# Split fp32r products for q, k, v, gate values and u in a decoder step, with the split input kept in scratch

## The reference

```
h = x * (1.0 + sc1) + sh1
z = h @ w_in
q, k, v, f, u, gv, ga, gg = split(z)         # 512, 512, 512, 8, 512, 512, 1024, 1024 columns
logf = log_sigmoid(f + b_f)
u = gelu(u);  gv = layernorm(gelu(gv))
a = fox(q, k, v, logf)                       # attention with forget gates, paged cache for the samples
gm = u * (ws @ gv + b_s)                     # spatial gate in chunks of 128 tokens
m = (sigmoid(ga) * (a @ w_ao) + sigmoid(gg) * (gm @ w_go)) @ w_o
x = layernorm(ALPHA * x + (1.0 + g1) * m)
out = layernorm(ALPHA * x + (1.0 + g2) * moe(x * (1.0 + sc2) + sh2))
```

## Time and profile before

| | |
|---|---|
| median of three runs | 1812.11 us (1808.1 to 1812.4) |
| the profiled execution, its own time | 1809.96 us |
| its span in the profile | 1807.8 us |
| mean granted TensorE clock | 0.944 |
| PE busy, DVE busy, ACT busy, POOL busy | 87%, 48%, 31%, 14% |
| modulate | 0 to 46 us |
| project_in | 46 to 300 us |
| gmlp | 304 to 385 us |
| attend | 389 to 880 us |
| mix | 882 to 1188 us |
| mixer_out, route, experts, combine | 1188 to 1808 us |

### The profile page before, as it was taken

The page is one execution under the profiler, slowest core; times in us unless marked ns, Lnnn a source line. Parts: engine busy times, 40 slices in busy tenths (PEclk is TensorE's granted clock), DMA queues, the critical chain, the costliest instruction groups (busy, mean ns, idle before and its releaser), DMA issues. The chain is left out here.

```text
span 1807.8 us, 32157 instructions
## 1 busy us (share of the span) xinstructions
PE 1580.4 (87%) x11702; PEld 1101.8 (61%) x11702; DVE 870.4 (48%) x1311; ACT 566.9 (31%) x965; POOL 244.2 (14%) x230
## 2 busy tenths in 40 slices
PE   5999998958999999998599998979952899999965
PEld 3444444647776767765399998944431567676731
DVE  2011111924565555555354645434344666766638
ACT  1000002102444444444234334300010556665622
POOL 0001010031001010000121313103231111111021
PEclk9999999978999999999699999989985999999987
DMA  8634443046999989996356464552113899999954
GB/s 331 236 119 166 156 154 94 18 160 229 362 326 322 335 296 334 310 306 208 102 134 186 124 183 124 139 199 70 47 50 143 316 378 419 419 418 418 404 186 183
DMA packets 226254, 411.60 MB, mean 228 GB/s; under 512 B 18844, under 2 KB 112221, under 8 KB 217942
## 3 DMA queue, kind: packets, MB, share of 16 engines
q1 hardware_dynamic: 208392, 345.44, 55.0%
q0 software_dynamic: 13152, 47.95, 7.4%
q10 hardware_dynamic: 4608, 16.78, 2.3%
HBM read 367.26 MB, written 42.85 MB: 227 GB/s over the span
## 5 line engine op out<-in xcount | busy, mean ns | idle before, releaser
L326 PE MATMUL ps<-w_w,h_hT 128*128 128x512 f32 x512 | 227.4, 603 | 7.5 <-issue 4.0
L1527 PE MATMUL ps<-mix_x_hi,mix_w_hi 128*128 128x352 f32 x576 | 188.5, 327 | 25.3 <-DVE mix_x_lo L1479 21.8
L2209 DVE TENSOR_TENSOR ex_w_lo<-we_w_gu,ex_w_hi 128x1024 fp32r<-128x1024 f32 x128 | 150.8, 1220 | 103.1 <-ACT ex_w_hi L2254 102.5
L1527 PE MATMUL ps<-mix_x_hi,mix_w_lo 128*128 128x352 f32 x576 | 187.2, 325 | 0.0
L1527 PE MATMUL ps<-mix_x_lo,mix_w_hi 128*128 128x352 f32 x576 | 186.5, 324 | 0.0
L326 PEld LDWEIGHTS ps<-w_w,h_hT 128*128 128x128 f32 x512 | 97.1, 192 | 126.7 <-issue 125.3
L2254 ACT CAST ex_w_hi<-we_w_gu 128x1024 fp32r<-128x1024 f32 x128 | 128.5, 1061 | 94.8 <-DMA we_w_gu<-w_exp_up 87.0
L976 PE MATMUL ps<-g_ident,at_k_pg 128*128 128x128 f32 x1024 | 140.8, 281 | 15.9 <-DVE at_kT L1163 15.8
L976 PEld LDWEIGHTS ps<-g_ident,at_k_pg 128*128 128x128 f32 x1024 | 115.5, 143 | 63.2 <-issue 38.6
L1569 DVE TENSOR_TENSOR mix_w_lo<-g_arena,mix_w_hi 128x1024 fp32r<-128x1024 f32 x73 | 125.7, 1753 | 41.0 <-ACT mix_w_hi L1554 28.1
L1163 ACT COPY at_kT<-ps 128x512 f32<-128x512 f32 x128 | 74.9, 585 | 179.1 <-PE ps L976 179.1
(11 more groups left out here) (386 smaller groups left out, 2337.0 us busy)
## 6 DMA issues: line engine op xcount, KB each, us to landing
at_k_pg<-cache_k SPq DMA_DIRECT2D x256, 256.0 KB, 4.1
at_v_pg<-cache_v SPq DMA_DIRECT2D x256, 256.0 KB, 4.2
we_w_gu<-w_exp_gate SPq DMA_DIRECT2D x32, 1024.0 KB, 8.9
we_w_gu<-w_exp_up SPq DMA_DIRECT2D x32, 1024.0 KB, 11.2
we_w_dn<-w_exp_down SPq DMA_DIRECT2D x32, 1024.0 KB, 8.1
g_arena<-w_in SPq DMA_DIRECT2D x49, 512.0 KB
h_extra<-w_ada SPq DMA_DIRECT2D x16, 1024.0 KB
y_rows<-ex_y ACTq DMA_DIRECT2D x32, 512.0 KB, 7.5
```

Of the source, the lines that this page charges most:

```text
L326: last = nc.tensor.matmul(ps[:, b, :], g.hT[:, k, t * P:(t + 1) * P], w[s][:, k, :], start=(k == 0), stop=(k == KD - 1))
L1527: last = nc.tensor.matmul(out, w[p][:, at], v[:, x, :], start=(i == 0 and k == 0), stop=(i == len(w_chunks) - 1 and k == 2))
L2209: nc.vector.tensor_tensor(w_lo[half][:, i], w_gu[s][:, i, half * KH:(half + 1) * KH, :], w_hi[half][:, i].bitcast(F32), ALU.subtract).then ...
```

## The change

**Operands.** An operand of a product is split on chip into `hi`, its value rounded to fp32r, and `lo`, the fp32 difference, itself rounded. An fp32 matmul `h @ w` becomes three fp32r matmuls: h_hi x w_hi, h_hi x w_lo and h_lo x w_hi. This is done for the prompt tiles of q, k, v and gv and for all of u. The sample tiles of the four groups stay one fp32 product of the raw operands. The forget logits stay fp32 and are computed as h_hi @ w_f + h_lo @ w_f, sixteen rounds of matmuls in place of eight.

**project_in.** `g.hT` becomes `g.h` with both parts; the lo part is written over the raw values (`twin` makes the same bytes visible in both types). ACT rounds h a tile at a time and the weights in four pieces of two chunks, DVE subtracts. The weights of the next group are split during the last four tiles of a group. The two weight buffers hold hi and lo, and u's weights are a fifth group that goes through them. `g.z` has two slots in place of four, so v waits for q's stores and gv for k's. The `Fori` loop is gone. The sample tile of a group is computed in the middle of the group before it, ahead of the split (that of q at the very start). SP issues the weights of group g+1 when the last tile of group g-1 is done. The ada rows are stored a piece at a time.

The core of the diff (renamings and moved buffers left out):

```diff
 # project_in, SP
-for it in range(2):
-    for s, (at, by) in enumerate(((COL_Q, COL_V - COL_Q), (COL_K, COL_GV - COL_K))):
-        if it or s:
-            sp.wait_ge(w_used[s], START + it)
-            sp.dma_start(w[s][:], w_v[:, :, it * by + at:it * by + at + 512]).then_inc(w_in[s], 16)
-        for a in range(A):
-            x, use, column = piece(it, s, a)
-            sp.wait_ge(ada_added[x], START + use)
-            sp.dma_start(ada_w[x][:, :, :], ada_v[:, :, bass.ds(2 * D + column, PIECE)]).then_inc(ada_in[x], 16)
...
+for gi in range(GROUPS):
+    s = (gi + 1) % 2
+    if gi:
+        sp.wait_ge(w_used[s], (gi + 1) // 2)
+    sp.dma_start(g.w_raw[s][:, 1], w_v[:, :, GROUP_COLS[gi + 1]:GROUP_COLS[gi + 1] + 512])\
+        .then_inc(w_in[s], 16)
+    for n in range(A * gi, A * gi + A):
+        x = n % 2
+        if n >= 2:
+            store_ada(n - 2)
+        sp.dma_start(ada_w[x], ada_v[:, :, 2 * D + n * PIECE:2 * D + (n + 1) * PIECE]).then_inc(ada_in[x], 16)
...
 # project_in, PE, a prompt tile
-for k in range(KD):
-    last = nc.tensor.matmul(ps[:, b, :], g.hT[:, k, t * P:(t + 1) * P], w[s][:, k, :],
-                            start=(k == 0), stop=(k == KD - 1))
+if gi == 0:
+    pe.wait_ge(h_lo_done, t + 1)
+for k in range(KD):
+    if t == 0 and k % 2 == 0:
+        pe.wait_ge(w_lo_done, CH * gi + k // 2 + 1)
+    for i, (h, w) in enumerate(((h_hi, w_hi), (h_hi, w_lo), (h_lo, w_hi))):
+        last = nc.tensor.matmul(ps[:, b, :], h[:, k, tokens(t)], w[:, k, :], start=(k == 0 and i == 0),
+                                stop=(k == KD - 1 and i == 2))
...
+if t % 2:
+    a = A * gi + t // 2
+    x = a % 2
+    pe.wait_ge(ada_in[x], 32 * (a // 2) + 32)
...
 # project_in, POOL
-for j in range(3):
-    pool.dma_start(g.hT_rows[:, j], g.hT[:, :, j * BLK:(j + 1) * BLK]).then_inc(out, 16)
+pool.wait_ge(h_lo_done, NT)
+for part, src in enumerate((h_hi, h_lo)):
+    for j in range(3):
+        pool.dma_start(g.hT_rows[part, :, j], src[:, :, j * BLK:(j + 1) * BLK]).then_inc(h_out, 16)
...
 # gmlp, PE, forget logits
-for j in range(3):
-    last = nc.tensor.matmul(ps[32 * j:32 * j + H, 6, 0:BLK], w_f[:, k, :],
-                            g.hT[:, k, j * BLK:(j + 1) * BLK], start=(k == 0), stop=(k == KD - 1))
+for part in range(2):
+    for j in range(3):
+        last = nc.tensor.matmul(ps[32 * j:32 * j + H, 6, 0:BLK], w_f[:, k, :],
+                                g.h[:, part, k, j * BLK:(j + 1) * BLK].bitcast(F32), start=(k == 0 and part == 0),
+                                stop=(k == KD - 1 and part == 1))
...
 # mix, POOL
+def load_h(j):
+    if j >= 2:
+        pool.wait_ge(w_used[1], START + KD * (j - 1))
+    for part in range(2):
+        pool.dma_start(h_x[j % 2][:, part], g.hT_rows[part, :, j]).then_inc(h_in[j % 2], 16)
 def block_start(j):
-    for q in (1, 2, 3):
-        split_lo(pool, nc.gpsimd.tensor_tensor, q, j)
+    split_lo(pool, nc.gpsimd.tensor_tensor, 1, j)
+    if j < 2:
+        load_h(j + 1)
```

More of the change, by code:

```diff
@@ L1 @@
+import math
 from contextlib import ExitStack
@@ L8 @@
 F32 = mybir.dt.float32
+F32R = mybir.dt.float32r
 I32 = mybir.dt.int32
@@ new lines, in evacuate @@
+            def evacuate(eng, copy, n):
+                gi, t = GROUP_TILES[n]
+                b, slot = n % 6, gi % 2
+                if gi == 2 and t in (0, 1, PT):
+                    eng.wait_ge(q_out, 16 * (1 + H // 2))
+                if gi == 3 and t in (0, 1, PT):
+                    eng.wait_ge(k_out, 16 * (2 + H // 2))
+                eng.wait_ge(full[b], n // 6 + 1)
+                if t == PT - 1:
+                    eng.sem_inc(w_used[gi % 2], 1)
+                if t < PT:
+                    last = copy(g.z[:, slot, t, :], ps[:, b, :])
+                else:
+                    for j in range(4):
+                        last = copy(g.z[0:NS, slot, t, j * P:(j + 1) * P], ps[NS * j:NS * j + NS, b, 0:P])
+                last.then_inc(free[b], 1)
@@ L375, in add_bias, with h_rest, w_rest @@
                     last.then_inc(ada_added[x], 1)
-                evacuate(dve, nc.vector.tensor_copy, 0, add_bias)
+                def h_rest(t):
+                    dve.wait_ge(h_hi_done, t + 1)
+                    nc.vector.tensor_tensor(h_lo[:, :, tokens(t)], raw(t),
+                                            h_hi[:, :, tokens(t)].bitcast(F32), ALU.subtract).then_inc(h_lo_done, 1)
+                def w_rest(gi, c):
+                    at = slice(2 * c, 2 * c + 2)
+                    if gi < GROUPS and c == 0:
+                        n = GROUP_TILES.index((gi, PT))
+                        dve.wait_ge(full[n % 6], n // 6 + 1)
+                    dve.wait_ge(w_hi_done, CH * gi + c + 1)
+                    nc.vector.tensor_tensor(g.w[gi % 2][:, 1, at], g.w_raw[gi % 2][:, 1, at],
+                                            g.w[gi % 2][:, 0, at].bitcast(F32), ALU.subtract).then_inc(w_lo_done, 1)
@@ new lines, in _ @@
+                w_rest(0, 0)
+                h_rest(0)
+                for c in range(1, CH):
+                    w_rest(0, c)
+                for t in range(1, 4):
+                    h_rest(t)
+                for n, (gi, t) in enumerate(GROUP_TILES):
+                    if n % 2 == 0:
+                        evacuate(dve, nc.vector.tensor_copy, n)
+                    if t == PT:
+                        continue
+                    if t % 2:
+                        add_bias(A * gi + t // 2)
+                    if gi == 0 and t + 4 < NT:
+                        h_rest(t + 4)
+                    if t >= PT - CH:
+                        w_rest(gi + 1, t - PT + CH)
@@ new lines, in _ @@
+                h_round(0)
+                for c in range(1, CH):
+                    w_round(0, c)
+                for t in range(1, 4):
+                    h_round(t)
+                for n, (gi, t) in enumerate(GROUP_TILES):
+                    if n % 2:
+                        evacuate(act, nc.scalar.copy, n)
+                    if t == PT:
+                        continue
+                    if gi == 0 and t + 4 < NT:
+                        h_round(t + 4)
+                    if t >= PT - CH:
+                        w_round(gi + 1, t - PT + CH)
@@ L385, in _, with pairs @@
                 tok = "(t p) n -> p t n"
-                def pairs(which, src):
+                def pairs(which, src, out):
                     for pair in range(H // 2):
@@ L1453, in steps @@
         def steps(eng, block_start, body):
-            with eng.Fori(0, 3) as j:
+            for j in range(3):
                 block_start(j)
```

325 lines of the change are left out of this document (166 added, 159 removed).

## The result

Before 1811.25 us (median, 1808.1 to 1812.8), after 1818.76 us (1813.7 to 1823.4); ratio 1.0038, 95% interval 1.0027 to 1.0049. The forecast was 1805, with a range up to 1818: the sign was wrong, and the time lies just outside the range. The profiled execution of after took 1818.91 us with a span of 1817.2 us.

The account below looks back on a forecast made before the run. The prediction took TensorE to bound project_in and mix inside a third, and VectorE gmlp; project_in -9, gmlp +3 and mix -1 gave -7 us, from the median 1812.11 to 1805 us, range 1766 to 1818.

Parts of the forecast that it names:

- the two starts in mix: Second and third starts in mix: h's share of the splitting goes, saving 3.4 + 2.4 less 1.5 for half clock: -4.3 us.
- The three waits: Project_in, groups 1 to 3: PE waits for the first ada piece, queued behind weights and sharing packets with stores: +31 us.
- T: In project_in, the end of group g-1, when SP issues the next weights and POOL begins to store.
- A: Rival: project_in's loads arrive in time because queues share otherwise than in the trace; 1768 us, 13%.
- B: Rival: project_in's queues share by bytes, waits of 6 us a group and one and a half clock losses less; 1789 us, 18%.
- The half clock behind them: Project_in: after each of the three waits PE runs on at a reduced clock, 2 us lost each: +6 us.
- Products of project_in: Prompt tiles in project_in: 24 fp32r steps at 0.2275 us replace fp32, 1.4 us saved a tile, 32 tiles: -45 us.
- Project_in in all: Whole stage: products -45, loop gone -5.7, start +4.5, waits +31, half clock +6, together -9 us.
- gmlp: Forget product's 24 more matmuls shift the stage by 4.8 us, faster u saves little, half clock +2: sum +3 us.
- mix: Whole stage: starts -4.3, h load at the first third +2, the other two loads +1.5: sum -1 us, between -7 and +6.
- Rival D: In mix, h loads' larger packets hold up gate pieces; each of three loads adds up to 5 us; 1825 us, 12%.
- Rival E: Fp32r with h stationary does not run at the experts' rate, or the waits are 13 us each; 1816 us, 15%.

Follow-up runs that it names:

- e1: Changed kernel with SP storing and loading a group's first ada piece before it waits to load the next group's weights in project_in; 1773.75 us, ratio 0.9794.
- e2: Changed kernel with GpSimd's stores of q, k and v held back until the next group's first ada piece has landed; 1783.53 us, ratio 0.9851.
- e5: Kernel of e2 with the stores of both parts of h also held back until ada piece 4 has landed; 1779.28 us, ratio 0.9807.
- e3: Changed kernel with the second gate's weights in mix split a step ahead, at the end of the step before; 1806.73 us, ratio 0.998.
- e7: Changed kernel with the mix stage of the kernel before, except that it loads h's upper part and splits it again; 1814.56 us, ratio 1.0012.
- e6: Kernel of e1 with each project_in prompt tile's 24 fp32r steps put back to 8 fp32 products on the upper parts alone; 1814.87 us, ratio 1.002.
- e10: Kernel with the edits of e1, e3 and e4 together, with the forget product in fp32r too; 1748.16 us, ratio 0.9643.
- e4: Changed kernel with the last four blocks of u placed ahead of gate-value tiles 2 to 4 in TensorE's order; 1808.82 us, ratio 0.9982.
- e9: Kernel with the edits of e1, e3 and e4 together, with mix loading the next third of h in four portions; 1745.62 us, ratio 0.9639.

## Why the prediction was wrong, step by step

The profiled execution was to have a span 7 us shorter and has one 9.4 us longer. Two steps failed with enough weight to turn the sign: the waits with the half clock behind them were put at 37 us and took 42.4, and the two starts in mix, where 4.3 us were to be saved, saved nothing, since PE's waits there and the half clock behind them took 13.5 us where 8.3 were put down. The other differences are smaller or lie in stages that the forecast left at zero.

- **The three waits: right in place and cause, 5 us too small.** 35.6 us against 31, the first 13.9 against 11, the others 10.7 and 11.0 against 10. The packet rule was only roughly right: SP had 149 GB/s beside the stores, not 110, and 727 packets against 1350 rather than one for one; but the piece still landed 26 us after T, where the forecast had 23. I had missed what the row at 108.25 shows, that SP's own issue is held up for 9 us (8.17 us at the same place in e1, where PE does not wait for it). Rivals A and B are out; e2 and e5 show the sharing, e1 the place in the queue.
- **The half clock behind them: 6.8 against 6** (7.4 and 7.6 in e3 and e7). Waits and clock together are 42.4 (e1) where the forecast had 37: 5.4 us of the miss, the largest single piece.
- **Products of project_in: 42 against 45 (e6).** The term took 24 steps at the experts' 0.2275. In the trace a steady step is 0.231 and the first of each tile 0.333, where the product moves on to another accumulator: 5.65 us a tile and not 5.46. That rate was read from the middle of a run in the earlier trace rows, which has no such boundary. On the other side an fp32 tile takes 6.97 us and not 6.9, which gives 2 us back. Against the kernel before, project_in without its waits (e1) is 258.1 - 212.4 = 45.7 us shorter, the loop's end included, where the terms -45 - 5.7 + 4.5 gave 46.2. That this sum fits is luck: in e1 the start cost 2.4 us where 4.5 was put down (PE idles 2.47 us ahead of tile 0, as forecast, but the first two tiles then lose 1.55 us against later ones, and before the change they lost 1.69), and the end of the stage gave 0.5 us; both made up for the products. (The forecast's "some 7 us lower" for the other rate is 24 x 32 x 0.0115 = 9 us.)
- **Project_in in all: -1.8 against -9.** The waits and the clock behind them are 5.4 us of the difference and the first sample tile at half clock 1.6, a thing of this execution that only e10 shows again.
- **gmlp: +2.7 against +3, right,** with the forget product's 5 us and the idle stretch of 9.2 us as forecast; the seven executions with this gmlp take 78.2 to 80.1 us, the one of before 77.0. e4 shows that the idle stretch was there to be filled.
- **mix: +3.2 against -1 in this execution, +1.5 on average (e7 and the runs beside it), the wrong sign.** The step that failed is the saving of 4.3 us at the two starts. The cause of the wait was seen: the subtraction for w_lo of gate piece 1 still falls beside POOL's and takes 4.17 us there (4.0 in the forecast). Its price was not: the forecast let PE wait 3.4 us at each start and put 1.5 us down for the half clock of both. PE waited 4.1 and 4.0 us and then ran some five microseconds at a granted clock of 0.50, so that a first step took 6.9 and 6.6 us more than a steady one, 13.5 in all against the forecast's 8.3. In the kernel before, a start (with the last step ahead of it, which was late there) cost 6.7 and 5.5 us more than steady steps, in e7 6.6 and 6.7. So h's share was gone and nothing got cheaper. And the load of h in the background cost 1.8 us, in one third of the two, where the forecast had 1.5 (after's second step is 13.37 us against 11.60; e9 takes such a delay away). Rival D, 5 us a load, was far too dear. The rows are of after: the third part's start, and the granted clock (after PE busy) behind the wait of the second.

```profile
1106.11 0.96 PE L1610 MATMUL ps<-mix_h_x,mix_w_hi 128*128 128x352 f32 x2 [4.00 <-DVE mix_w_lo L1656]
```

```profile
1006.00:1012.00 6.00, 5.50 (x19) 0.50 0.94 332
```

- **Rival E** had the right order of size by two wrong reasons: the waits near 12 us each and fp32r slower than the experts' rate were each half true. Together with mix they are the outcome, so a time near its 1816 does not bear it out.
- **What is left.** -1.8 + 2.7 + 3.2 = +4.1 us, against 4.9 to 8.9 measured. The profile of after is 9.4 us longer: it has 2.5 us more in front of attend, where the first product waits for a load of `new_v_sample` (13.0 us, 10.7 before), and 1.2 us more ahead of project_in, which starts at 47.2 us (46.1 before, 45.2 to 47.0 in the other runs). The remainder, a microsecond or less each, lies in attend and behind mix. The gap before attend is 11.6 to 16.5 us in kernels whose code is the same there, but 13.1 or more in eleven of the twelve, against 12.0 in the one profile of before. Whether the change has a part in it is open.

The error was small terms with the same sign, with a range whose top (1818) left out that the waits, the clock and mix could miss together.

## What to carry to other kernels

Before a load is put behind another in one queue, add up what the queue must move between the event that releases both and the use of the second, at the rate that it gets beside the stores which the same event releases; if the second is small and its buffer is free earlier, issue it first: here one swapped order was worth 42 us in its stage and 45 in the medians, all that the faster products had brought. Read a rate across the boundaries that the new code will have (a tile, a bank), not from the middle of a run. And where an engine idles for a chain on another, look in its own program for work that needs nothing of that chain, before making either faster.

## What the runs showed of the hardware

- **More than one pace at full clock.** With a granted clock of 1.00 and TensorE busy all the time, the same matmuls of 352 columns keep one pace for long stretches of one execution and another in the next. After, nine steps each: 1.45 us at 1030 us, 1.42 us at 1150 us. A step of mix takes 11.44, 11.52 or 11.60 us by that, up to 1.4% apart, and which thirds have which differs from run to run: 24 steps can differ by 4 us with the same code. The cause is open.

```profile
1029.94 0.49 PE L1610 MATMUL ps<-mix_h_x,mix_w_hi 128*128 128x352 f32 x2
...
1031.39 0.48 PE L1610 MATMUL ps<-mix_h_x,mix_w_hi 128*128 128x352 f32 x2
...
1150.00 0.48 PE L1610 MATMUL ps<-mix_o_x,mix_w_hi 128*128 128x352 f32 x2
...
1151.42 0.48 PE L1610 MATMUL ps<-mix_h_x,mix_w_hi 128*128 128x352 f32 x2
```

- **VectorE beside GpSimd.** A subtraction of 1024 columns takes 1.21 us alone and 4.17 us beside a subtraction of 1408 columns on GpSimd (4.04 us). I had taken it for a slowdown by a factor; the ends of the two rows show one waiting for the other. The Trainium skill ("SBUF — State Buffer", SBUF: two separate sides) says that the two engines share a pair of ports as "an exclusive lock, not a bandwidth split". The rows agree: 1.1 us from POOL's end to DVE's, against 1.21 alone. In e3, having gate piece 1 ready before that moment was worth 10 to 14 us of mix.
